# First products of a sublayer: the shift as two columns beside the rounded residual, remainder products 256 columns wide

## The reference, cut to what matters

```
def norm_mod(h, j):
    shift = mod[:, j, 0][:, None, :]
    scale = mod[:, j, 1][:, None, :]
    return _rms(h) * g_norm[l, j] * (1.0 + scale) + shift
...
gu = h @ w_up                 # feed-forward: then silu(g) * u, then @ w_down
proj = h @ w_in               # mixer: then recurrences and attentions, then @ w_out
x = x + gate(j) * (...)
```

## Time and profile before

| | us |
|---|---|
| median of 3 runs | 1554.44 |
| lowest, highest | 1553.84, 1556.49 |
| span of the profiled execution | 1551.5 |
| median less that span | 2.9 |
| TensorE matmul busy | 1531.4 (99%) |
| VectorE busy | 1294.4 (83%) |
| ScalarE busy | 911.6 (59%) |

### The profile page before, as it was taken

How to read it: one execution, slowest core, us unless ns; L and a number is a source line. 1 busy time by engine, 2 the same in 40 slices (tenths; PEclk the granted TensorE clock), 3 DMA queues, 4 the chain that set the end, 5 groups by cost and what they waited for, 6 DMA issues and landing times.

```text
span 1551.5 us, 32204 instructions
## 1 busy us (share of the span) xinstructions
PE 1531.4 (99%) x13130; PEld 1512.1 (97%) x13130; DVE 1294.4 (83%) x1943; ACT 911.6 (59%) x1584; POOL 282.0 (18%) x288
## 2 busy tenths in 40 slices
PE   6999999999999999999999999999999999999998
PEld 6999999999999999999999999999999999999998
DVE  7998898997898888888998889889888889885553
ACT  6555468765555545459765455677555466765453
POOL 4322000112210222000113242101222201021100
PEclk9999999999999999999999999999999999999999
DMA  9999974479987899864579998445999963567761
GB/s 366 363 375 335 316 254 163 164 251 324 321 319 265 300 312 324 300 231 164 177 251 332 314 335 286 150 137 164 321 329 332 332 233 123 167 207 239 239 209 42
DMA packets 110612, 401.99 MB, mean 259 GB/s; under 512 B 12450, under 2 KB 12706, under 8 KB 110336
## 3 DMA queue, kind: packets, MB, share of 16 engines
q1 hardware_dynamic: 109136, 395.34, 73.2%
q0 software_dynamic: 1328, 4.58, 0.9%
HBM read 398.83 MB, written 1.05 MB: 258 GB/s over the span
## 4 chain that ended last, share of the span: by engine, by line
PE 88%; DVE 5%; ACT 4%; DMA 1%; issue 1%; DVEq 0%; SPq 0%; ACTq 0%
PE PS L626 87%; DVE WL L1909 2%; ACT WH L1373 1%; DMA ring<-in_up 1%; DVE SCR L1909 1%; DVE SCR L1912 1%; DVE SCR L2293 1%; DVE SMALL L2292 0%; ACT SCR L1701 0%; DVE ring L1935 0%; DMA ring<-in_ada 0%; PE PS L1215 0%; PE PS L827 0%; DVE SMALL L2332 0%; ACT HH L1405 0%
## 5 line engine op out<-in xcount | busy, mean ns | idle before, releaser
L1909 DVE TENSOR_TENSOR WL<-ring,WH 128x1024 fp32r<-128x1024 f32 (+1 forms) x502 | 603.5, 1236 | 151.9 <-ACT WH L1373 151.4
L626 PE MATMUL PS<-HH,WH 128*128 128x256 f32 (+2 forms) x2600 | 617.6, 279 | 1.9 <-DVE WL L1909 1.2
L626 PE MATMUL PS<-HL,WH 128*128 128x256 f32 (+1 forms) x2592 | 602.1, 277 | 0.0
L1373 ACT ACTIVATE WH<-ring 128x1024 fp32r<-128x1024 f32 (+1 forms) x502 | 507.0, 1050 | 44.2 <-PE PS L626 36.0
L626 PEld LDWEIGHTS PS<-HH,WH 128*128 128x128 f32 (+1 forms) x2600 | 488.2, 188 | 3.8 <-issue 2.6
L626 PEld LDWEIGHTS PS<-HL,WH 128*128 128x128 f32 x2592 | 481.1, 188 | 0.5
L626 PE MATMUL PS<-HH,WL 128*128 128x256 f32 (+1 forms) x2592 | 372.0, 277 | 0.4
L1935 DVE CUSTOM_DVE_ANT_0 ring<-ring,CB,VC 128x1024 f32<-128x1024 f32 x240 | 331.3, 1397 | 3.2 <-DMA ring<-in_ada 3.2
L626 PEld LDWEIGHTS PS<-HH,WL 128*128 128x128 f32 x2592 | 332.1, 188 | 1.3 <-DVE WL L1909 1.1
L626 PE MATMUL PS<-AH,WH 128*128 128x256 f32 x1056 | 292.4, 277 | 0.0
L626 PE MATMUL PS<-AH,WL 128*128 128x256 f32 x1056 | 292.1, 277 | 0.2 <-DVE WL L1909 0.2
(11 more groups left out here) (257 smaller groups left out, 1535.0 us busy)
## 6 DMA issues: line engine op xcount, KB each, us to landing
ring<-in_up SPq DMA_DIRECT2D x176, 512.0 KB, 5.7
ring<-in_ada SPq DMA_DIRECT2D x144, 512.0 KB, 6.1
ring<-in_ffn SPq DMA_DIRECT2D x132, 512.0 KB, 4.9
ring<-in_mod SPq DMA_DIRECT2D x96, 512.0 KB, 6.0
ring<-in_down SPq DMA_DIRECT2D x88, 512.0 KB, 5.8
ring<-in_win SPq DMA_DIRECT2D x64, 512.0 KB, 5.5
ring<-in_wout SPq DMA_DIRECT2D x32, 512.0 KB, 4.4
ring<-in_winv SPq DMA_DIRECT2D x8, 512.0 KB, 4.2
```

The source lines that it names most:

```text
L626: return e.matmul(out, lhsT, rhs, start=start, stop=stop, skip_group_check=skip)
L1373: e.activation(half_of(i)[0], slot_of(("half", i, 0))[:, 0:w], ACT.Copy).then_inc(s_hi, 1)
L1909: return e.tensor_tensor(out, a, b, op)
```

## The change

The shift's rounded part stands in column 256 of `HH` and its remainder in column 257 of `HH`, and nothing in columns 256 and 257 of `HL`. The 258-column products with `HL` are 256 columns wide and write columns 0 to 255 of the output only; those with `HH` stay 258 wide. The result's columns 256 and 257 are then W^T times the rounded shift and W^T times its remainder, and VectorE adds the two when it takes them out of PSUM: a `tensor_reduce` over two columns instead of a `tensor_copy` of one. ScalarE's copy of the shift is 8 elements per partition instead of 16, and so is VectorE's subtraction. No semaphore, no wait and no order changes.

```
 early(n, p, b):
-    out = PS[:, b, 0:S + 2]
+    out, own = PS[:, b, 0:S + 2], PS[:, b, 0:S]
...
         mm(out, wh[:, k, :], HH[:, k, 0:S + 2], start=k == 0, stop=False)
-        mm(out, wh[:, k, :], HL[:, k, 0:S + 2], start=False, stop=False)
+        mm(own, wh[:, k, :], HL[:, k, 0:S], start=False, stop=False)
...
 early_pair(n):
+    owns = [PS[:, 2 + p, 0:S] for p in range(2)]
...
-        mm(outs[p], whs[p][:, k, :], HL[:, k, 0:S + 2], start=False, stop=False)
+        mm(owns[p], whs[p][:, k, :], HL[:, k, 0:S], start=False, stop=False)
...
 gained(m, c) on ScalarE:
-    shift = MOD[:, 24 * m:24 * m + 8].rearrange("p (k o) -> p k o", o=1).to_broadcast([128, KD, 2])
-    e.activation(HH[:, :, S:S + 2], shift, ACT.Copy)
+    shift = MOD[:, 24 * m:24 * m + 8].rearrange("p (k o) -> p k o", o=1)
+    e.activation(HH[:, :, S:S + 1], shift, ACT.Copy)
...
 gained(m, c) on VectorE:
-    tt(HL[:, :, S:S + 2], shift, HH[:, :, S:S + 2].bitcast(F32), ALU.subtract)
+    tt(HH[:, :, S + 1:S + 2], shift, HH[:, :, S:S + 1].bitcast(F32), ALU.subtract)
...
 early(n, u, out) on VectorE:
-    e.tensor_copy(SM_[:, 160 + 2 * u:162 + 2 * u].rearrange("p (a o) -> p a o", o=1), b[:, :, S:S + 1])
+    e.tensor_reduce(SM_[:, 160 + 2 * u:162 + 2 * u], b[:, :, S:S + 2], AX.X, ALU.add)
```

More of the change, by code:

```diff
@@ L782, in early_pair @@
                     mm(outs[p], whs[p][:, KD - 1, :], HH[:, KD - 1, 0:S + 2], start=False, stop=False)
-                    mm(outs[p], whs[p][:, KD - 1, :], HL[:, KD - 1, 0:S + 2], start=False, stop=False)
+                    mm(owns[p], whs[p][:, KD - 1, :], HL[:, KD - 1, 0:S], start=False, stop=False)
                 sum_squares(n)
```

## The result

| | us |
|---|---|
| kernel before, median of 4 runs | 1555.47 |
| changed kernel, median of 4 runs | 1571.80 (1571.00 to 1572.48) |
| ratio, with its 95% interval | 1.0112 (1.0100 to 1.0124) |
| span of the profiled execution, before and after | 1551.5 and 1570.7 |

A forecast was written before the change was run, and what follows sets the result against it. TensorE, busy 99% of the span, was taken to bound the kernel. Its 1.58 us of savings less 0.02 us for the reductions gave 1.56 us, so 1552.9 us against 1554.44; range 1551.3 to 1555.6 us.

The forecast's parts named there:

- The bound: Whole kernel: TensorE, busy 99% of the span and 88% of the chain of waits, sets the time.
- the sum over the narrowed products alone: First products of n = 1 to 9: 288 narrowed products save at most 2.19 us, of which 1.58 us count.
- The prediction's own last sign of being wrong: Outside the first products: the prediction is wrong if the time of all other parts moves by more than these do.
- 7.6 ns for each narrowed product: Remainder products in the first products: starts 120.9 ns apart at 258 columns, 113.3 ns at 256, so 7.6 ns saved each.
- the rivals of the alternation: Pairs in p = 1 and 2: 242 ns means width changes eat the gain (17%), 247 that they cost more (6%).
- rivals 1 to 3: First products: width changes eat the gain, 1554.4 us (17%); cost 13 ns each, 1556.0 (6%); only columns count, 1554.2 (7%).
- Rival 2: First products: each change back to 256 columns costs 13 ns, 1.56 us more in all, 1556.0 us; chance 6%.
- The line through the widths: TensorE products of 128, 256 and 512 columns: some 7 ns on top up to 256, 13 to 17 ns from 258.
- n = 2 and 5 gain nothing: Feed-forwards after the first mixer: TensorE, 0.24 us earlier, waits 0.24 us for VectorE's normalised remainders; nothing counted.
- The small operations: VectorE's 18 reductions 160 ns instead of 150, 0.02 us later in the chain; ScalarE's shift copy and VectorE's subtraction count nothing.
- The median from the span: Whole kernel: 2.9 us between profiled span and median added to the forecast span of 1549.9 us, giving 1552.9 us.
- The chances: Whole kernel, change of over 0.2% (3.1 us): faster 5%, same 92%, slower 3%.

The follow-up runs named there:

- the last version above: Changed kernel, narrow products behind the first products of n = 1 to 9 removed, five added in the last output product, those ahead of f = 3 kept: 1552.95 us.
- the first version's 12 runs: Changed kernel without any narrow product in n = 1 to 9, with five in the last output product: median 1551.35 us, 4 runs at 1556.69 to 1557.38.

## Why the prediction was wrong, point by point

- **The bound.** "What shortens the stream of products shortens the time" was right, and so was reading distances of starts. Its other side was not used: 4.4 ns more at each of some 4100 products costs 18 us, eight times all that the change could gain.
- **The step that failed** is the sum over the narrowed products alone: the price of all other products was taken as the fixed 113.3 ns of the long streams. The trace of before had a second distance for the same form, for which the sum has no term: its last output product runs at 117.8 ns from chunk 3 on, and parts of the output products of n = 1 and 4 do. The prediction's own last sign of being wrong, that parts outside the first products move by more than these, came true: 20 us there, against 1.2 us in the first products. The run without the narrow product at the exit (1554.19 us) and the one with full weights (1552.98 us) differ from the changed kernel by a single kind of instruction and have none of the loss.
- **7.6 ns for each narrowed product.** The first products of n = 3 take 501.58 - 489.73 = 11.85 us now, 12.03 before: 0.18 us for 32 products, 5.6 ns each instead of 7.6. The 23 distances of p = 3 take 501.47 - 498.73 = 2.74 us (forecast 2.72, before 2.78), and the stretch of n = 1 up to the weight remainder at 225.05 is 0.14 us shorter (forecast 0.2). The pairs of p = 2 in n = 3:

```profile
495.87 0.28 PE L626 MATMUL PS<-HH,WH 128*128 128x258 f32 x1
496.00 0.28 PE L626 MATMUL PS<-HL,WH 128*128 128x256 f32 x1
...
497.76 0.40 PE L626 MATMUL PS<-HH,WL 128*128 128x258 f32 x2
```

  8 pairs in 1.89 us are 236 ns; forecast 234, with 241 or more for the rivals of the alternation. So the cost does belong to the instruction for the most part, and rivals 1 to 3 are wrong in their mechanism. Rival 2 had the right side and, by chance, the right place, the exit. It put the price on each change of width, where it lies on what follows.
- **The line through the widths** The earlier trace rows was weaker than it was made. The 0.06 us for 128 columns is read from a pair that stands behind products of 384 columns. Where 128-column products follow each other, the same trace has 0.11 us from start to start (eight in 1.05 us, less the 0.28 us of the last, over 7 distances), so "some 7 ns on top up to 256 columns" does not hold for them. The step from 256 to 258 columns is shown by the change itself, by the 5.6 ns.

```profile
1002.34 1.05 PE L626 MATMUL PS<-SCR 128*128 128x128 f32 x8
```

- **n = 2 and 5 gain nothing.** TensorE was to arrive early and wait, the eight products taking 1.3 us. In the changed kernel n = 5 shows 1.21 and n = 2 no wait, since it had lost 0.3 us ahead of that. In the last version above, without the narrow product at the exit, it is plain in n = 2: 1.40 us, at 322.09.

- **The small operations.** The reduction takes 153 ns (forecast 160, the copy 150). The subtraction takes 175 ns at 8 elements as it did 176 at 16, ScalarE's copy 217 ns:

```profile
L1987 DVE TENSOR_REDUCE SMALL<-PS 128x2 f32<-128x4 f32 x18 | 2.8, 153 | 0.0
L1910 DVE TENSOR_TENSOR HH<-MOD,HH 128x8 fp32r<-128x8 f32 x9 | 1.6, 175 | 3.9 <-ACT HH L1387 3.9
...
L1386 ACT ACTIVATE HH<-MOD 128x8 fp32r<-128x8 f32 x9 | 1.9, 217 | 18.7 <-DVE X L1913 18.7
```

- **The median from the span.** The 2.9 us around the span were the difference to the median of other runs. Runs whose span is listed show 1.8 us (1572.48 against 1570.7), so the profiled execution of before took about 1553.3 us.
- **The chances.** Slower by over 0.2% had 3%. The sizes of the parts bounded only what the changed instructions do themselves. In a kernel where more than 10,000 products of one width stand behind each other, a change next to the stream should have had a case for the stream itself.

What stays open: what state of TensorE the two distances stand for, and why a product with 4 weight columns selects the slow one behind alternating widths, lifts it within the slow stream of a feed-forward, and does nothing within a fast one or behind 258-column products. Four kernels with the same narrowed first products and the narrow product behind them have 6 of 9, 9 of 9, 6 of 6 and 6 of 9 slow exits, and the exits of n = 4 and n = 6 change sides between them, so the code of the exit alone does not settle it.

## What to carry to other kernels

Where one engine's stream sets the time, count the instructions per stretch in both profiles before anything else: a busy share of 100% at full clock hid 4% here. A row that shows the same form of instruction at two distances in the trace of before is a warning that a change next to the stream may flip it, and that case deserves a chance of its own. A product with few weight columns in a stream of full ones is not only its 0.12 us: try the change with it and without it.

## What the runs showed of the hardware

- A stream of products of 128 weight columns and 256 columns of fp32r ran at 113.3 or 117.8 ns from start to start, at granted clock 1.00 in both, and kept either for up to 1488 products.
- One product of 4 weight columns (its load shows 0.09 us instead of 0.19) was followed by the fast distance in each of the 13 places in feed-forwards where it met a slow stream (ahead of f = 3 or 12, in seven kernels). Directly behind first products with alternating 258 and 256 columns it left the slow one in 27 of 33 places; without it, or with 128 weight columns, none of the 30 such exits was slow.
- It is no cure in itself. In the output products of n = 1 and 4 it stands behind four transposes, and there the stream was slow ahead of them and slow behind it in all 15 profiles. In the kernel before, 27 distances of n = 1 take 3.18 us on either side, 117.8 ns each:

```profile
290.35 0.28 PE L626 MATMUL PS<-YH,WH 128*128 128x256 f32 x1
...
293.53 0.28 PE L626 MATMUL PS<-YH,WH 128*128 128x256 f32 x1
...
294.24 0.36 PE L626 MATMUL PS<-YH,WF 128*4 128x256 f32 x1
294.43 0.28 PE L626 MATMUL PS<-YH,WH 128*128 128x256 f32 x1
...
297.61 0.28 PE L626 MATMUL PS<-YH,WH 128*128 128x256 f32 x1
```

  In those of n = 6 and 8 of the changed kernel the stream behind such a product ran slow for 11 us, where it had been fast.
- A stop for data can set either distance, and can leave it. Stops of 0.3 us turned a fast stream slow in n = 5 of one profile and n = 2 of another, and left it fast in n = 2 of the first; going by the times, it happened in 4 of the first version's 12 runs. Of the shorter ones (eight products in 1.21 to 1.23 us) four turned a slow stream fast, in n = 2 or 5 of three kernels, two left it slow, the two of the version with p = 3 wide turned a fast one slow, and one of the version with the five further products left it fast. A stop for a weight remainder inside the output product of n = 5 was followed by the fast distance in the kernel before and by the slow one in the kernel that is narrow in p = 3 only. In n = 7 the last 15 us of the output product ran slow in five of the 15 profiles (not in those of the kernel before and the changed one) behind no stop at all: no distance there is over 0.12 us.
- In the last output product of the kernel before, each of the five pairs of transposes behind chunks 2 to 6 was followed by a chunk at the slow distance; a narrow product right behind the pair was followed by the fast one (46 or 47 products in 5 us instead of 45).
